# A fused 1-core fp32 block kernel: the orders of the mixer on VectorE and ScalarE, and output products taken ahead on two attention tiles

## The chip, the cores and the metric

The kernel runs on one core of one Trainium2 chip. The metric is device time in microseconds (us) of one execution; the number to compare is the median of several runs. A core has five engines with queues of their own: TensorE (PE in the profile; its weight loads are PEld), VectorE (DVE), ScalarE (ACT), GpSimd (POOL) and SyncE (SP, which here only issues DMAs). Each engine works through its queue in order; an instruction that waits for a semaphore holds back all that stands behind it on its engine.

## The reference

Two blocks in a row, all in float32, batch 1, 256 tokens, width 1024. The first block is a gated delta-net layer, a banded attention layer and two convolutional feed-forward layers. The second block, on which the change works, is one layer with a mixer and an MLP:

```
h = modulate(rmsnorm(x), sh1, sc1)
rq, rk, rv, rg, aq, ak, av = split(h @ w_in)            # w_in: 1024 x 2816
ret = silu(rg) * groupnorm(bidir_retention(rope(rq), rope(rk), rv)) * g   # 4 heads of 128
att = attention(rope(rms(aq)), [ctx keys, rope(rms(ak))], [ctx values, av])  # 8 heads of 64, 512 keys
x = x + g1 * (concat([ret, att]) @ w_out)               # w_out: 1024 x 1024
h2 = modulate(rmsnorm(x), sh2, sc2)
x = x + g2 * (relu(h2 @ w_ff1)**2 @ w_ff2)              # 1024 x 4096, 4096 x 1024
```

The result is a last rmsnorm of x.

## The kernel before

**Weights.** A weight matrix is cut in units of 128 x 1024 numbers (512 KB). For each unit SP issues a DMA into one of four `raw` slots; ACT copies it into one of four `wH` slots as fp32r (`hi`, L1362); DVE subtracts to get the remainder `wL` (`lo`, L2200). Every product is made of three matmuls, high x high, low x high and high x low (`three`, L607 to L609). `hi(c)` waits until PE has finished unit c - 4 (`unit_done`), and SP's DMA for unit c waits until `lo(c - 4)` is done. `ahead_hi(u)` and `ahead_lo(u)` are these two steps for unit u of the mixer, written by hand into the queues of ACT and DVE. Units 0 to 21 are `w_in`; units 22 to 29 are the eight units of `w_out` (`wo_c`, in the order of `OUT_UNITS`: pairs of bank j and half s, where s = 1 is the attention half of the rows of `w_out` and s = 0 the retention half); after them comes `w_ff1`.

**The mixer** (`win_pe`, `win_act`, `win_dve`) runs the projection with `w_in` and, between its units, four pairs of attention heads, p = 0 to 3, and four retention heads. One pair goes round the engines so: PE makes the scores (L1117); DVE takes the maxima (L2762); ACT the exponentials (L1725); DVE the reciprocals (L2771), and ACT and DVE each scale probabilities with them (L1732, L2775: `probabilities`); PE turns the probabilities (L1133, `att_turn`, 16 transposes); ACT and DVE copy them out of PSUM, ACT the upper and DVE the lower half (`probs_turned`: L1542 and L2780, into `stage` and `cv`); PE multiplies with the values (L1145, `att_y`); ACT and DVE split the result in high and low (`att_hi` L1542 into `yH`, `att_lo` L2200 into `zL`). DVE also makes the rotation of retention's keys and queries (`rotate`, L2743 to L2748), weights its scores (`ret_weights`, L2797) and sums its outputs (`ret_out`, L2802 to L2808), which PE makes in `ret_scores` (L1155) and `ret_outputs` (L1167, L1171).

**The end of the mixer.** Retention's outputs `o_r` get a group norm and the gate silu(rg) in `sg`. ACT: `ret_stats("square")` (L1763), the silu (L1856, which needs another activation table), `ret_stats("scale")` (L1765). POOL: an inverse root, the product of `sg` with the norm's gain in two parts (L2158), another inverse root. DVE: `last_stats`, `ret_stats("rows")` (L2829), `last_rows` (L2856). Then PE turns the rows (`ret_turn(0)` and `ret_turn(1)`, L1047) and ACT and DVE split them (`ret_hi`, `ret_lo`).

**The output product** (`mixer_out`) has eight units of 24 matmuls of 256 columns. `residual` (DVE, L2332, L2340) and `projected` (ACT, L1438) take each of its four banks, gate it and add it to x; `turn_pair` (PE, L769) turns two feature tiles of the new x, and ACT and DVE make `nH` and `nL` of them (L1383, L2253), the input of `w_ff1`. `OUT_DONE` says after how many units each bank is full. The first block of `w_ff1` (L1315 to L1317) waits for `nH` and `nL` pair by pair, and turns the fourth pair itself. The queue of PE, in order, ends the mixer with `att_turn(3)`, `att_y(3)`, then `mixer_out`.

Of the kernel before, what the change touches and what calls it, by code (L numbers as in the profile page):

```python
# [142 lines left out]
OUT_DONE = (3, 4, 6, 8)  # L143
OUT_UNITS = ((0, 1), (1, 1), (0, 0), (1, 0), (2, 1), (2, 0), (3, 1), (3, 0))
# [20 lines left out]
RET_OUT = (2, 2, 2, 1)  # L165
ATT_PAIR = ((4, 5), (6, 7))
# [66 lines left out]
def build(nc, a, out):  # L233
    with ExitStack() as ctx:
# [261 lines left out]
        s_tact = sem("s_tact")  # L496
        s_tdve = sem("s_tdve")
# [104 lines left out]
        def _(pe):  # L602
# [437 lines left out]
            def ret_turn(part):  # L1040

                pe.wait_ge(y_rows, part + 1)
                pe.wait_ge(m_od, 3 + part)
                for f in range(2):
                    for t in range(TT):
                        o = f * SEQ + t * P
                        tr = nc.tensor.transpose(ps[2 + part][:, o:o + P], o_r[:, t, DECAYS[2 * part + f]], ident)  # L1047
                tr.then_inc(y_pe, 1)

            def win_pe(X, C):  # L1050
# [85 lines left out]
                def att_y(p):  # L1136

                    pe.wait_ge(s_tact, 2 * p + 2)
                    pe.wait_ge(s_tdve, 2 * p + 2)
# [102 lines left out]
                att_turn(3)  # L1242
                att_y(3)

# [41 lines left out]
            win_pe(X, [xcH, xcL])  # L1286
            pe.wait_ge(m_od, RET_H)

            def mixer_out(x):
                b = {}  # L1290
                for u, (j, s) in enumerate(OUT_UNITS):
                    if u == 0:
                        pe.wait_ge(y_ready, RET_Y)
                    elif u == 2:
                        pe.wait_ge(y_ready, RET_Y + 2)
                    if s == 1:
                        b[j] = bank("wo_c", 0, j)
                    for t in range(TT):
                        token_half(b[j], 0, U("wo_c") + u, x, 1 - s, s, t)
                        if (u, t) == (0, 1):  # L1300
                            ret_turn(0)
                        elif (u, t) == (1, 0):
                            ret_turn(1)
                    if u in (4, 5, 7):
                        pair = (4, 5, 7).index(u)
# [45 lines left out]
        def _(act):  # L1351
# [65 lines left out]
            def projected(name):  # L1417
# [11 lines left out]
                for j in range(4):  # L1429
# [5 lines left out]
                    if j < 3:  # L1435
                        act.wait_ge(unit_done, U(name) + OUT_DONE[j])
                        act.wait_ge(unstaged, STAGED[name] + j - 1)
                        fn(stage[:, (STAGED[name] + j) % 2].rearrange("p a b -> p (a b)"), ps[(BANK[name] + j) % 4][:],  # L1438
                           ACT.Copy).then_inc(bank_free, 1)
                        ahead(0, U(name) + 2 * j)  # L1440
# [250 lines left out]
            def win_act():  # L1691
# [42 lines left out]
                def probs_turned(p):  # L1734
                    for g in range(2):
                        act.wait_ge(s_turn, 4 * p + 2 * g + 2)
                        cp(apT[g][:, 2:4].rearrange("p a b -> p (a b)"), ps[ATT_PAIR[g][1]][:]).then_inc(s_tact, 1)
# [1536 lines left out]
```

## Time and profile before

| | us |
|---|---|
| three runs | 1031.83, 1034.03, 1032.27 |
| median | 1032.27 |
| the profiled execution | 1034.53 |
| its span in the trace | 1032.7 |
| busy PE | 996.9 (97%) |
| busy DVE | 848.2 (82%) |
| busy ACT | 609.7 (59%) |
| busy POOL | 100.2 (10%) |

The time of the profiled execution is its span and 1.8 us around it. In the span the mixer's attention and retention lie at about 745 to 816 us, the output product at 816 to 842 us, `w_ff1` and `w_ff2` behind it. A row of the timeline gives the start, the busy time, the instruction, and in brackets how long the engine had been idle before it and what released it. The busy time of a matmul contains a modelled tail: matmuls of 256 columns start 0.12 us apart and show 0.28 us each, so a wait costs up to 0.16 us more than its bracket.

### The profile page before, as it was taken

The page shows a single profiled execution, that of the slowest core. Times are in us where ns is not written, and L with a number is a line of the kernel's source. Part 1 is how long each engine was busy: PE and PEld are TensorE (multiplying, and loading weights), DVE is VectorE, ACT ScalarE, POOL GpSimd, SP SyncE. Part 2 cuts the span into 40 slices and gives each one's busy share as a digit, 9 for nine tenths or more (in the row PEclk, how much of TensorE's full clock was granted, in tenths as well). Part 3 has the DMA queues.
Part 4 walks back from the last instruction along what each step waited for, and adds up shares of the span by engine and source line. Part 5 has one row for each costly group of instructions (what it writes and reads, how often), then busy time and mean ns, then how long its engine had stood idle before and what let it go on. Part 6 is the DMA issues. An engine that isn't in the chain of part 4 may idle for free.

```text
span 1032.7 us, 20800 instructions
## 1 busy us (share of the span) xinstructions
PE 996.9 (97%) x7662; PEld 925.4 (90%) x7662; DVE 848.2 (82%) x1566; ACT 609.7 (59%) x1056; POOL 100.2 (10%) x115
## 2 busy tenths in 40 slices
PE   6999999999999999998999999999998899999996
PEld 6999998999998889988999998888776799998884
DVE  5899888999889979887898899777788886668856
ACT  6697534766665564575766656556374565555443
POOL 1014422000000000001000001001200200000001
PEclk9999999999999999999999999999999999999998
DMA  9674313877776858737897757834422167766852
GB/s 292 171 212 154 103 55 104 247 210 211 224 213 217 292 165 266 268 100 235 224 274 208 220 185 257 272 100 135 132 70 75 42 162 206 221 196 220 278 149 116
DMA packets 216194, 193.09 MB, mean 187 GB/s; under 512 B 6032, under 2 KB 193568, under 8 KB 216000
## 3 DMA queue, kind: packets, MB, share of 16 engines
q1 hardware_dynamic: 206560, 158.09, 51.6%
q0 software_dynamic: 9136, 33.51, 9.8%
q8 instruction: 41, 0.67, 0.3%
q10 hardware_dynamic: 432, 0.61, 0.2%
q14 instruction: 25, 0.20, 0.1%
HBM read 191.14 MB, written 1.06 MB: 186 GB/s over the span
## 4 chain that ended last, share of the span: by engine, by line
PE 77%; DVE 12%; ACT 5%; DMA 3%; issue 2%; POOL 0%; POOLq 0%; ACTq 0%; DVEq 0%
PE ps L607 21%; PE ps L609 20%; PE ps L608 20%; DVE wL L2200 3%; PE ps L1316 3%; PE ps L1317 3%; PE ps L1315 3%; DMA modw<-in_w_mod_t 1%; DVE cv L3002 1%; PE ps L888 1%; ACT wH L1362 1%; DMA raw<-in_f_w_up 1%; PE ps L1145 1%; PE ps L875 1%; PE ps L784 1%
## 5 line engine op out<-in xcount | busy, mean ns | idle before, releaser
L1362 ACT ACTIVATE wH<-raw 128x1024 fp32r<-128x1024 f32 x298 | 313.5, 1062 | 260.4 <-PE ps L609 197.8
L2200 DVE TENSOR_TENSOR wL<-raw,wH 128x1024 fp32r<-128x1024 f32 x298 | 358.2, 1228 | 61.9 <-ACT wH L1362 61.0
L607 PE MATMUL ps<-yH,wH 128*128 128x256 f32 x704 | 195.3, 277 | 1.0 <-DVE yL L2253 1.0
L608 PE MATMUL ps<-yL,wH 128*128 128x256 f32 x704 | 194.4, 276 | 0.0
L609 PE MATMUL ps<-yH,wL 128*128 128x256 f32 x704 | 194.4, 276 | 0.0
L607 PEld LDWEIGHTS ps<-yH,wH 128*128 128x128 f32 x704 | 132.1, 188 | 1.3 <-DVE yL L2253 1.2
L608 PEld LDWEIGHTS ps<-yL,wH 128*128 128x128 f32 x704 | 132.2, 188 | 0.1
L609 PEld LDWEIGHTS ps<-yH,wL 128*128 128x128 f32 x704 | 132.1, 188 | 0.0
L607 PE MATMUL ps<-wH,aH 128*128 128x512 f32 (+1 forms) x308 | 119.4, 388 | 0.7 <-DVE aL L2200 0.6
L609 PE MATMUL ps<-wH,aL 128*128 128x512 f32 (+1 forms) x308 | 119.1, 387 | 0.0
L608 PE MATMUL ps<-wL,aH 128*128 128x512 f32 (+1 forms) x308 | 119.0, 386 | 0.0
L607 PE MATMUL ps<-wH,xH 128*128 128x256 f32 (+1 forms) x304 | 94.0, 309 | 3.2 <-DVE xL L2200 2.3
L608 PE MATMUL ps<-wL,xH 128*128 128x256 f32 (+1 forms) x304 | 91.6, 301 | 0.0
L609 PE MATMUL ps<-wH,xL 128*128 128x256 f32 (+1 forms) x304 | 91.6, 301 | 0.0
L3067 DVE SCALAR_TENSOR_TENSOR cv<-stage,cols,cv 128x254 f32<-128x254 f32 (+1 forms) x176 | 73.3, 481 | 1.5 <-ACT cv L1935 1.5
L607 PE MATMUL ps<-xH,wH 128*128 128x256 f32 x256 | 72.2, 282 | 0.8 <-DVE xL L2253 0.8
L1316 PE MATMUL ps<-nL,wH 128*128 128x256 f32 x256 | 72.6, 283 | 0.0
L1315 PE MATMUL ps<-nH,wH 128*128 128x258 f32 x256 | 72.2, 282 | 0.0
L1317 PE MATMUL ps<-nH,wL 128*128 128x258 f32 x256 | 72.1, 282 | 0.0
L608 PE MATMUL ps<-xL,wH 128*128 128x256 f32 x256 | 71.7, 280 | 0.0
L609 PE MATMUL ps<-xH,wL 128*128 128x256 f32 x256 | 71.7, 280 | 0.0
L2035 POOL DMA_DIRECT2D modw<-in_w_mod_t x48 | 25.9, 540 | 469.4 <-DVE modc L2222 326.8
(430 smaller groups left out, 2176.8 us busy)
## 6 DMA issues: line engine op xcount, KB each, us to landing
raw<-in_f_w_up SPq DMA_DIRECT2D x88, 512.0 KB, 5.0
raw<-in_w_ff SPq DMA_DIRECT2D x64, 512.0 KB, 4.7
modw<-in_w_mod_t POOLq DMA_DIRECT2D x48, 512.0 KB, 5.1
raw<-in_f_w_down SPq DMA_DIRECT2D x44, 512.0 KB, 4.4
raw<-in_a_w_in SPq DMA_DIRECT2D x32, 512.0 KB, 4.9
raw<-in_w_in SPq DMA_DIRECT2D x22, 512.0 KB, 3.8
raw<-in_w_kv SPq DMA_DIRECT2D x16, 512.0 KB, 5.4
raw<-in_a_w_out SPq DMA_DIRECT2D x8, 512.0 KB, 3.5
```

Of the source, the lines that this page charges most:

```text
L607: mm(o, l[0], r[0], start=first, stop=False, skip_group_check=check)
L608: mm(o, l[0], r[1], start=False, stop=False, skip_group_check=check)
L609: return mm(o, l[1], r[0], start=False, stop=last, skip_group_check=check)
L784: tr = nc.tensor.transpose(ps[first + k // 2][:, o:o + P], rows[:, t, k * P:(k + 1) * P], ident)
L875: tr = nc.tensor.transpose(ps[bank][:, x * P:(x + 1) * P], T_[:, 4 * g + x], ident)
L1315: mm(o[:, 0:SEQ + 2], w[0][:, k], nH[:, k, 0:SEQ + 2], start=k == 0, stop=False, skip_group_check=True)
L1316: mm(o[:, 0:SEQ], w[0][:, k], nL[:, k], start=False, stop=False, skip_group_check=True)
L1317: return mm(o[:, 0:SEQ + 2], w[1][:, k], nH[:, k, 0:SEQ + 2], start=False, stop=k == KD - 1, skip_group_check=True)
L1362: fn(slot(wH, c), raw[:, c % RAW], ACT.Copy).then_inc(hi_done, 1)
L2035: pool.dma_start(mod_tile(m), a["w_mod_t"][m * P:(m + 1) * P, :]).then_inc(mod_in[m % MOD_RING], 16)
L2200: return tt(o, x, hi.bitcast(F32), ALU.subtract)
L3067: c = stt(o[:, d:], x[:, 0:SEQ - d], w, o[:, d:], ALU.mult, ALU.add)
```

## The change

It changes no arithmetic, only orders, banks and which engine copies. Part by part:

- On DVE `probabilities(0)` stands before the rotation (`rotate(512, 0, 1)`), and `probabilities(2)` before `ahead_lo(22)`; on ACT `probabilities(2)` stands before `ahead_hi(23)`.
- For pair 1 ACT copies all four turned quarters; DVE copies none.
- On ACT the silu with its table load stands behind `ret_stats("square")` and `probs_turned(3)`; `ahead_hi(25)` stands before `att_hi(3)`, and `ahead_hi(26)` and `ahead_hi(27)` are taken into the mixer, before `ret_hi(0)` and `ret_hi(1)`. On DVE `ahead_lo(25)` stands before `last_rows`, `ahead_lo(26)` between `ret_lo(0)` and `ret_lo(1)`, and `ahead_lo(27)` behind them.
- On PE the first three units of `w_out` all belong to the attention half. Their products with the attention tiles that pairs 0 and 1 made (tiles 0 and 2 of the half: 12 of a unit's 24 matmuls) are taken ahead (`first_out`): one unit's before `att_y(3)`, two behind it. `mixer_out` makes the other half of each (tiles 1 and 3) and then the retention half, with new banks (`OUT_BANKS`, `RET_TURNED`) and new waits.
- The banks are full after 4, 5, 6 and 8 units (before: 3, 4, 6 and 8), and `turn_pair(0)` and `turn_pair(1)` each come one unit later.

```diff
-OUT_DONE = (3, 4, 6, 8)
-OUT_UNITS = ((0, 1), (1, 1), (0, 0), (1, 0), (2, 1), (2, 0), (3, 1), (3, 0))
+OUT_DONE = (4, 5, 6, 8)
+OUT_UNITS = ((0, 1), (1, 1), (2, 1), (0, 0), (1, 0), (2, 0), (3, 1), (3, 0))
+OUT_BANKS = (0, 2, 1, 3)
+OUT_AHEAD = ((6, 7), (8,), (9,))
+RET_TURNED = (5, 7)
...
+            def out_products(u, t, x, tiles):
+
+                j, s = OUT_UNITS[u]
+                w = [y.rearrange("p (k n) -> p k n", k=4) for y in w_unit(0, 8, U("wo_c") + u)]
+                for k in tiles:
+                    last = three(ps[OUT_BANKS[j]][:, t * 256:(t + 1) * 256],
+                                 [y[:, 4 * s + k, t * P:(t + 1) * P] for y in x], [y[:, k] for y in w],
+                                 s == 1 and t == 0 and k == 0, s == 0 and k == (1 if u == 3 else 3), check=True)
+                return last
+
+            def first_out(u, x):
+
+                for t in range(TT):
+                    out_products(u, t, x, (0, 2))
...
                 ret_outputs(3)
                 att_turn(3)
+                pe.wait_ge(m_od, 3)
+                pe.wait_ge(y_ready, ATT_Y + 4)
+                first_out(0, Z)
                 att_y(3)
+                first_out(1, Z)
+                pe.wait_ge(m_od, RET_H)
+                first_out(2, Z)
...
             def mixer_out(x):
...
+                pe.wait_ge(y_ready, RET_Y)
+                for u in range(3):
                     for t in range(TT):
+                        last = out_products(u, t, x, (1, 3))
+                        if (u, t) == (1, 1):
+                            last.then_inc(unit_done, 1)
                             ret_turn(0)
+                        elif (u, t) == (2, 0):
                             ret_turn(1)
+                    if u != 1:
+                        last.then_inc(unit_done, 1)
+                for part, tiles in ((0, (2, 3)), (1, (0, 1))):
+                    pe.wait_ge(y_ready, RET_Y + part + 1)
+                    for t in range(TT):
+                        last = out_products(3, t, x, tiles)
+                last.then_inc(unit_done, 1)
+                for u in range(4, 8):
+                    for t in range(TT):
+                        last = out_products(u, t, x, range(4))
+                    last.then_inc(unit_done, 1)
+                    if u >= 5:
+                        pair = u - 5
                         pe.wait_ge(unstaged, STAGED["wo_c"] + pair + 1)
                         turn_pair(pair, AUX + pair)
...
                 def probs_turned(p):
                     for g in range(2):
+                        if p == 1:
+                            act.wait_ge(s_turn, 4 * p + 2 * g + 1)
+                            cp(apT[g][:, 0:2].rearrange("p a b -> p (a b)"), ps[ATT_PAIR[g][0]][:]).then_inc(apt_low, 1)
                         act.wait_ge(s_turn, 4 * p + 2 * g + 2)
```

On VectorE, at the turned probabilities of pair 1: the queue before, from the end of the rotation of the first 128 tokens (`wt` and `qk_t` are its operands) to the next one.

```order
L2747 TENSOR_TENSOR qk_t<-qk_t,wt 128x4x64
L2748 TENSOR_TENSOR qk_t<-qk_t,wt 128x4x64
L2780 COPY stage<-ps 128x512
L2780 COPY cv<-ps 128x512
L2743 TENSOR_TENSOR wt<-qk_t,tb 128x256
```

The same place of the changed kernel:

```order
L2781 TENSOR_TENSOR qk_t<-qk_t,wt 128x4x64
L2782 TENSOR_TENSOR qk_t<-qk_t,wt 128x4x64
L2777 TENSOR_TENSOR wt<-qk_t,tb 128x256
L2778 TENSOR_TENSOR wt<-qk_t,tb 128x256
L2779 TENSOR_TENSOR qk_t<-qk_t,tb 128x4x64
```

The two copies are gone from DVE's queue; on ACT each of `stage` and `cv` is copied twice at that place.

On ScalarE, at the end of the mixer: before, from the last exponentials (`ap_`) on.

```order
L1725 ACTIVATE ap_,st_p<-ps,st_p 128x512 x2
L1856 ACT_TABLE_LOAD
L1856 ACTIVATE sg<-sg 128x1024
L1763 ACTIVATE rope,st_r<-o_r,st_r 128x128 x4
L1542 ACTIVATE stage<-ps 128x512
L1542 ACTIVATE cv<-ps 128x512
L1542 ACTIVATE yH<-ps 64x256 x2
L1362 ACTIVATE wH<-raw 128x1024
L1765 ACTIVATE o_r<-o_r,st_r 128x128 x4
L1542 ACTIVATE yH<-ps 128x512 x2
```

And in the changed kernel:

```order
L1795 ACTIVATE rope,st_r<-o_r,st_r 128x128 x4
L1571 ACTIVATE stage<-ps 128x512
L1571 ACTIVATE cv<-ps 128x512
L1890 ACT_TABLE_LOAD
L1890 ACTIVATE sg<-sg 128x1024
L1390 ACTIVATE wH<-raw 128x1024
L1571 ACTIVATE yH<-ps 64x256 x2
L1797 ACTIVATE o_r<-o_r,st_r 128x128 x4
L1390 ACTIVATE wH<-raw 128x1024
L1571 ACTIVATE yH<-ps 128x512
L1390 ACTIVATE wH<-raw 128x1024
L1571 ACTIVATE yH<-ps 128x512
```

The silu has moved behind the copies of the turned probabilities, and three weight copies now stand in front of splits (`yH`).

On TensorE, at the same time: before, from the last transposes of the probabilities (the names carry the bank numbers) on.

```order
L1133 MATMUL ps7<-cst,ap_ 128x128 x4
L1145 MATMUL ps4<-stage,cakv 64x256
L1145 MATMUL ps6<-cv,cakv 64x256
```

And in the changed kernel, where twelve rows of products with bank 0 lie between the transposes and `att_y(3)`, of which the first three and the last stand here:

```order
L1150 MATMUL ps7<-cst,ap_ 128x128 x4
L610 MATMUL ps0<-wH,yH 128x256
L611 MATMUL ps0<-wL,yH 128x256
L612 MATMUL ps0<-wH,zL 128x256
...
L612 MATMUL ps0<-wH,zL 128x256
L1162 MATMUL ps4<-stage,cakv 64x256
L1162 MATMUL ps6<-cv,cakv 64x256
```

What PE did last it does later now: `att_y(3)` stands behind half of unit 0's first pass.

## Rows read from the trace of the kernel before

**Rows 1.** Busy us (instructions) by stretch: PE, PEld, DVE, ACT, POOL; PE clock, DMA share, GB/s.
```profile
745.00:843.00 98.00, 90.12 (x653) 75.49 (x652) 78.76 (x162) 59.57 (x128) 5.39 (x4) 1.00 0.26 77
843.00:950.00 107.00, 107.00 (x838) 104.29 (x838) 75.18 (x139) 57.41 (x87) 3.83 (x5) 1.00 0.71 202
```
**Rows 2.** Timeline of PE, 749 to 830 us: each place where it stood idle.
```profile
754.62 1.97 PE L1133 MATMUL ps<-cst,ap_ 128*128 128x128 f32 x16 [0.68 <-ACT ap_ L1732]
...
779.04 0.40 PE L1145 MATMUL ps<-stage,cakv 128*64 128x256 f32 x1 [1.51 <-DVE cv L2780]
...
792.25 1.97 PE L1133 MATMUL ps<-cst,ap_ 128*128 128x128 f32 x16 [1.39 <-ACT ap_ L1732]
794.05 1.06 PE L1167 MATMUL ps<-rv,sT 128*128 128x128 f32 x8
...
808.95 1.97 PE L1133 MATMUL ps<-cst,ap_ 128*128 128x128 f32 x16 [0.31 <-DVE ap_ L2775]
812.71 0.43 PE L1145 MATMUL ps<-stage,cakv 128*64 128x256 f32 x1 [1.79 <-ACT cv L1542]
...
816.14 0.35 PE L607 MATMUL ps<-wH,yH 128*128 128x256 f32 x1 [1.49 <-issue]
816.33 0.28 PE L608 MATMUL ps<-wL,yH 128*128 128x256 f32 x1
816.46 0.28 PE L609 MATMUL ps<-wH,zL 128*128 128x256 f32 x1
...
829.58 0.35 PE L607 MATMUL ps<-wH,yH 128*128 128x256 f32 x1 [0.70 <-ACT stage L1438]
```
**Rows 3.** Timeline of DVE, 777 to 795 us: the copies of pair 1, the probabilities of pair 2.
```profile
778.22 0.68 DVE L2780 COPY cv<-ps 128x512 f32<-128x512 f32 x1
...
785.75 0.69 DVE L2791 COPY rqT<-ps 128x512 f32<-128x512 f32 x1 [0.88 <-PE ps L1095]
...
789.53 1.22 DVE L2200 TENSOR_TENSOR wL<-raw,wH 128x1024 fp32r<-128x1024 f32 x1
790.66 0.16 DVE L2771 RECIPROCAL st_p<-st_p 128x2 f32<-128x2 f32 x1
...
792.95 0.61 DVE L2808 SCALAR_TENSOR_TENSOR o_r<-ps,dec,o_r 128x128 f32<-128x128 f32 x2
```
**Rows 4.** Timeline of ACT, 774 to 813 us: pair 1's copies, pair 2's probabilities, the silu, pair 3's copies.
```profile
774.31 0.59 ACT L1542 ACTIVATE stage<-ps 128x512 f32<-128x512 f32 x1
...
777.56 0.60 ACT L1542 ACTIVATE sg<-ps 128x512 f32<-128x512 f32 x1 [1.23 <-PE ps L609]
...
790.85 1.34 ACT L1732 ACTIVATE ap_<-ap_,st_p 128x512 f32<-128x512 f32 x2 [0.58 <-DVE st_p L2771]
...
807.79 1.28 ACT L1856 ACT_TABLE_LOAD   x1
809.09 1.06 ACT L1856 ACTIVATE sg<-sg 128x1024 f32<-128x1024 f32 x1
...
812.07 0.58 ACT L1542 ACTIVATE cv<-ps 128x512 f32<-128x512 f32 x1
```
**Rows 5.** Timeline of DVE, 811 to 847 us: the end of the mixer and the last split.
```profile
811.03 0.68 DVE L2780 COPY cv<-ps 128x512 f32<-128x512 f32 x1
...
815.17 0.88 DVE L2200 TENSOR_TENSOR zL<-ps,yH 64x256 fp32r<-64x256 f32 x2 [0.18 <-ACT yH L1542]
...
819.04 1.14 DVE L2856 SCALAR_TENSOR_TENSOR o_r<-o_r,st_r,sg 128x128 f32<-128x128 f32 x4 [0.30 <-POOL st_r L2019]
820.09 1.22 DVE L2200 TENSOR_TENSOR wL<-raw,wH 128x1024 fp32r<-128x1024 f32 x1
...
822.19 0.69 DVE L2200 TENSOR_TENSOR zL<-ps,yH 128x512 fp32r<-128x512 f32 x1 [0.28 <-ACT yH L1542]
...
846.07 0.88 DVE L2253 SCALAR_TENSOR_TENSOR nL<-ps,gs,nH 128x256 fp32r<-128x256 f32 x2
```
**Rows 6.** Timeline of POOL, 813 to 818 us: the gain on the silu.
```profile
814.51 3.36 POOL L2158 TENSOR_TENSOR sg<-sg,rows_c 128x512 f32<-128x512 f32 x2
```

More of the change, by code:

```diff
@@ L1046, in ret_turn, with win_pe @@
                         o = f * SEQ + t * P
-                        tr = nc.tensor.transpose(ps[2 + part][:, o:o + P], o_r[:, t, DECAYS[2 * part + f]], ident)
+                        tr = nc.tensor.transpose(ps[RET_TURNED[part]][:, o:o + P], o_r[:, t, DECAYS[2 * part + f]], ident)
                 tr.then_inc(y_pe, 1)
-            def win_pe(X, C):
+            def out_products(u, t, x, tiles):
[9 more added lines that the diff above has]
+                    out_products(u, t, x, (0, 2))
+            def win_pe(X, C, Z):
                 bw = BANK["win"]
@@ L1437, in projected @@
                         act.wait_ge(unstaged, STAGED[name] + j - 1)
-                        fn(stage[:, (STAGED[name] + j) % 2].rearrange("p a b -> p (a b)"), ps[(BANK[name] + j) % 4][:],
+                        fn(stage[:, (STAGED[name] + j) % 2].rearrange("p a b -> p (a b)"), ps[OUT_BANKS[j]][:],
                            ACT.Copy).then_inc(bank_free, 1)
-                        ahead(0, U(name) + 2 * j)
+                        for c in OUT_AHEAD[j]:
+                            hi(0, 8, U(name) + c)
                     else:
@@ L1844, in win_act @@
                 exps(2, 0)
+                probabilities(2)
                 ahead_hi(23)
-                probabilities(2)
                 ahead_hi(24)
@@ L2340, in residual @@
                     tt(hc, hc, s, ALU.add).then_inc(unstaged, 1)
-                    if j < 3:
-                        ahead(0, U(name) + 2 * j)
+                    for c in OUT_AHEAD[j] if j < 3 else ():
+                        lo(0, 8, U(name) + c)
                     if j == 1:
@@ L2888, in win_dve @@
                 ahead_lo(17)
+                probabilities(0)
                 dve.wait_ge(bank_free, bw + 11)
                 rotate(512, 0, 1)
-                probabilities(0)
                 ahead_lo(18)
@@ L2917, in win_dve @@
                 ret_weights(1)
+                probabilities(2)
                 ahead_lo(22)
-                probabilities(2)
                 ret_out(0)
@@ L2937, in win_dve @@
                 ret_stats("rows")
+                ahead_lo(25)
                 last_rows()
-                ahead_lo(25)
                 ret_lo(0)
+                ahead_lo(26)
                 ret_lo(1)
+                ahead_lo(27)
             def by_tiles(gate):
```

44 lines of the change are left out of this document (15 added, 29 removed).

## The prediction

> **What bounds the kernel now.** I read the busy times by stretch first. PE is busy in all 107 us of the stretch behind the mixer and the output product, and in 90.1 of the 98 us of the mixer and the output product themselves, at a granted clock of 1.00, which is 2.4 GHz, in both [rows 1]. So PE sets the time, and what can be won without less work is the idle time between 745 and 843 us. The timeline of PE shows where it lies [rows 2]: seven places, with brackets of 0.68, 1.51, 1.39, 0.31, 1.79, 1.49 and 0.70 us, 7.9 us together, which is all but 0.1 us of the idle time in the window (98.00 - 90.12 = 7.88). Each bracket names an order on ACT or DVE: something less urgent stood before the instruction that PE needed. As PE never waits in the next 107 us, whatever PE gains here moves all that follows, and the weights, since their transfers are released by PE's progress through `unit_done` and `lo_done`; I take it through to the end at full value.
>
> How to price one wait: where the same kind of matmul goes on, it costs its bracket and the 0.16 us of modelled tail (starts 0.12 us apart, 0.28 us shown). Where PE changes into or out of `att_y`, the change alone costs about as much, and I take the bracket.
>
> **The change part by part.**
>
> *Pair 0.* The reciprocals come before a rotation of six instructions, so ACT's scaled probabilities are there before the products with `ckv` end, and the 0.68 us wait goes: 0.68 + 0.16 = 0.84. The rotation that steps back is needed by PE only for the transposes at some 766 us, and what DVE did next was a weight split; nothing is late in its place.
>
> *Pair 1.* The wait of 1.51 us at 779.04 ends with DVE's copy into `cv`, 778.22 + 0.68 = 778.90 [rows 2, 3]. That copy stood behind a rotation. On ACT the four copies cost at most 4 x 0.6 = 2.4 us from 774.31 [rows 4], so the last ends before 776.7, and PE is ready at 779.04 - 1.51 = 777.5: hidden with 0.8 us to spare. Behind them on ACT come one weight copy and the copy of `sg`, which had 1.23 us of idle time before it [rows 4], as much as the two new copies take. All 1.5 us are won.
>
> *Pair 2.* The wait of 1.39 us at 792.25 costs 1.39 + 0.16 = 1.55. DVE split a weight unit (789.53) before its reciprocal (790.66): 1.13 us [rows 3]. With the order turned, ACT's two scalings start 1.13 us earlier than 790.85 [rows 4], the transposes at 791.12, and end at 792.92. But PE's next step, `ret_outputs(1)` (794.05 in the rows, directly behind the transposes), needs DVE's `ret_out(0)`, which ends at 792.95 + 0.61 = 793.56 [rows 3] and does not move, since the weight split is only put behind the reciprocals and still lies before it. So PE starts it at about 793.6 instead of 794.05 [rows 2]: of 1.13 us only 0.45 arrive, and a new wait of 0.6 us for `o_r` appears. That DVE is otherwise no further behind is seen in its own wait for PE of 0.88 us just before [rows 3]: it moves with PE.
>
> *Pair 3, before the transposes* (0.31 us): scores, maxima and exponentials keep their order; it stays.
>
> *Pair 3, behind the transposes.* PE waits 1.79 us, until 812.71, for ACT's copy that starts at 812.07 [rows 2, 4]. ACT had loaded a table for 1.28 us, made the silu for 1.06 us and then four squares. DVE's own copy, 811.03 + 0.68 = 811.71 [rows 5], is the next that is late: moving the silu alone wins 1.0. With `first_out(0)` PE has 12 matmuls x 0.12 = 1.4 us of products at hand from 810.75 to 812.2, and DVE's copy is hidden too. Won: 1.7. The 1.28 us and 1.06 us of the silu now start at about 811.5, so `sg` is ready at 813.9. POOL takes it at 814.51 [rows 6], behind an inverse root of its own: 0.6 us of slack, so it costs nothing.
>
> Here a rule of the Trainium skill speaks against the change. The table load of 1.28 us ends at 809.07, and the silu starts at 809.09 [rows 4]: nothing lies between. "ScalarE: Activation LUTs", section "Rules for kernel authors", wants about 2.7 us counted for each switch to another table set; by it the silu would be ready 1.4 us later, POOL 0.8 us later, and the sum below about 0.3 us smaller. The row decides.
>
> *The seam into the output product.* PE waits 1.49 us at 816.14 for the end of DVE's split, 815.17 + 0.88 = 816.05 [rows 2, 5]. With `first_out(1)` and `first_out(2)`, 24 x 0.12 = 2.8 us, PE is busy until about 817. Won: 1.5.
>
> *The bank wait at 829.58* (0.70 + 0.16 = 0.86): PE waited because units 26 and 27 were split only after the first bank had been staged. They are now split in the mixer. Won: 0.86.
>
> *What it costs.* (a) Three more changes between kinds of matmul: the first of a kind starts its successor 0.19 us later instead of 0.12 (816.14 to 816.33, against 816.33 to 816.46 [rows 2]), and the change itself about 0.1: 0.4 together, between 0.2 and 0.8. (b) `ahead_lo(25)` now stands before `last_rows`, which therefore end at 819.04 + 1.14 + 1.1 = 821.3 instead of 820.2 [rows 5]; PE arrives at `ret_turn(1)` at about 821.2 (808.95 + 1.8 transposes + 1.4 + 1.9 `att_y` + 2.8 + 3.6 products of the second pass + 0.4 turn + 0.3 changes). So 0.2, between 0 and 1. Behind it, `ret_lo(1)` ends about 823.4 (before: 822.88 [rows 5]), with one more weight split in front of it, and PE needs it at 823.7. (c) Banks 0 and 1 are full, and turned, one unit later (24 x 0.12 = 2.8 us), so ACT and DVE carry four banks' work in less time before the first block of `w_ff1`. The last `nL` was done at 846.07 + 0.88 = 846.95 [rows 5], just when PE came to it. I give it 0.4, between 0 and 2.
>
> **The sum.** 0.84 + 1.5 + 0.45 + 1.7 + 1.5 + 0.86 = 6.85 won, 0.4 + 0.2 + 0.4 = 1.0 lost: 5.8 us faster. Against the profiled execution, 1034.53 - 5.8 = 1028.7; that one is 2.3 us over the median, so against the median 1032.27 - 5.8 = **1026.5 us**.
>
> **Rivals.**
>
> *DVE becomes the bound at the end of the mixer.* For it: from 809 to 823 us DVE has only brackets of 0.18, 0.30 and 0.28 us [rows 5], it gets one weight split more before `ret_lo(1)`, and PE has only 0.3 us of slack to it. Each us by which `last_rows`, POOL's product or the front of `w_ff1` is later is a us lost. With the upper ends of (a), (b) and (c), 0.8 + 1 + 2 instead of 1.0, the gain is 3.0: **1029.3 us**.
>
> *More goes than I count.* Pair 2's new wait and the 0.31 us of pair 3 vanish because DVE has two copies (1.2 us) less to do, and (b) and (c) cost nothing: 6.85 + 1.1 + 0.3 - 0.3 = 8.0: **1024.3 us**.
>
> *The gain stays in the mixer.* If transfers, not PE, paced `w_ff1` (DMA share 0.71 [rows 1]), PE would wait there for what it gained. Against it: no idle time at all in that stretch. It would give **1031 us**, no change to be told.
>
> *Slower, by one thing in PE's queue.* `ret_turn(1)` waits for `last_rows`, and behind it on PE stand half a unit of ready products and all of unit 3. `last_rows` now stand behind `ahead_lo(25)`, that behind ACT's `ahead_hi(25)`, and this behind the silu. Each us that this chain is late beyond 821.2 stops PE for one us. It must be 5.8 + 2.1 = 7.9 us late before the kernel is slower than can be told, 1034.5 us or more. For it: four engines meet there. Against it: the pieces are single rows of 1.0 to 1.2 us, and unit 25's weights come long before.
>
> **How the numbers follow.** Forecast (gain 4 to 7.4) 0.60; DVE bound at the end (gain 2.1 to 4) 0.15; more goes 0.12; the gain stays in the mixer, or is eaten up, 0.08; slower 0.05. A measurement of this kernel can tell some 0.2%, 2.1 us, from no change. So faster 0.87, same 0.08, slower 0.05. The range that holds 8 in 10 reaches from a gain of 8.3 to one of 2.3: 1024.0 to 1030.0.
>
> **What would show it.** In the changed profile: no wait for `cv` from DVE at the `att_y` of pair 1; at pair 2 a shorter wait for `ap_` and a new one of about 0.6 us for `o_r` before `ret_outputs(1)`; products with `yH` between the last transposes and `att_y(3)`, and no wait before either; no wait for ACT's `stage` in the output product; perhaps 0.2 us before `ret_turn(1)` and 0.4 us for `nL` in the first block of `w_ff1`. The stretch behind stays fully busy. The prediction would be wrong if PE waits over 1 us at `ret_turn(1)`, at unit 3 or at the front of `w_ff1`, or if idle time shows up in `w_ff1` or `w_ff2` where there was none.

## The result, and the profile after

| | before | after |
|---|---|---|
| median of the runs beside each other, us | 1032.75 (4 runs) | 1027.18 (4 runs) |
| lowest and highest | 1031.83 and 1034.03 | 1026.71 and 1027.98 |
| ratio after to before, 95% interval | | 0.994 (0.9929 to 0.9952) |
| the profiled execution | 1034.53 | 1027.24 |
| its span | 1032.7 | 1025.4 |

The kernel is 5.6 us, 0.5 to 0.7%, faster; 1026.5 us was predicted. A second, later set of runs gave 1025.95 us (6 runs) against 1033.23 (11 runs), a ratio of 0.9931 (0.9918 to 0.9945).

The busy times by stretch of the changed kernel answer to [rows 1] (columns as there):

```profile
745.00:843.00 98.00, 96.81 (x718) 82.84 (x715) 84.08 (x172) 64.51 (x140) 7.59 (x5) 1.00 0.30 89
843.00:950.00 107.00, 107.00 (x806) 102.89 (x806) 75.13 (x137) 56.88 (x82) 2.88 (x6) 1.00 0.73 215
```

Of 7.88 us of idle PE 1.19 us are left, and the stretch behind is as full as before. The timeline of PE in the changed kernel, in answer to [rows 2]:

```profile
787.52 1.97 PE L1150 MATMUL ps<-cst,ap_ 128*128 128x128 f32 x16 [0.25 <-ACT ap_ L1761]
790.12 1.13 PE L1184 MATMUL ps<-rv,sT 128*128 128x128 f32 x8 [0.63 <-DVE o_r L2842]
...
805.09 1.97 PE L1150 MATMUL ps<-cst,ap_ 128*128 128x128 f32 x16 [0.30 <-DVE ap_ L2809]
806.81 0.37 PE L610 MATMUL ps<-wH,yH 128*128 128x256 f32 x1
...
808.40 0.43 PE L1162 MATMUL ps<-stage,cakv 128*64 128x256 f32 x1
...
810.27 0.38 PE L610 MATMUL ps<-wH,yH 128*128 128x256 f32 x1
...
817.20 0.60 PE L1049 MATMUL ps<-cst,o_r 128*128 128x128 f32 x4
...
838.90 0.38 PE L1343 MATMUL ps<-nH,wH 128*128 128x258 f32 x1
...
846.14 0.59 PE L630 MATMUL ps<-rd,cst 128*128 128x256 f32 x2
```

Three brackets are left in this stretch, and all three were named in the prediction: 0.25 (the shorter wait of pair 2), 0.63 (the new one for `o_r`) and 0.30 us (pair 3, which stays). The products with `yH` stand at 806.81 and 810.27, before and behind `att_y(3)`, without a bracket.

**A ruler for all runs.** Executions differ by a us or more in places that the change doesn't touch: the scores of pair 0 begin at 745.44 us before, at 744.33 after, and at 745.36 in a second profile of the changed kernel. So I measure from there in two pieces: **A**, from the first scores of pair 0 (L1117, L1134) to the transposes of pair 3 (L1133, L1150), and **B**, from these to the transposed roots in the first block of `w_ff1` (L627, L630). Before, A runs from 745.44 to 808.95 [rows 2] and B to 854.26; after, from 744.33 to 805.09 and 846.14.

| kernel | A, us | B, us | A + B | against after | median of its runs | ratio to before (95%) |
|---|---|---|---|---|---|---|
| before | 63.51 | 45.31 | 108.82 | +7.01 | 1032.75 to 1033.4 (five sets) | |
| after | 60.76 | 41.05 | 101.81 | | 1027.18 | 0.994 (0.9929 to 0.9952) |
| `e11_changed_again` | 60.76 | 41.06 | 101.82 | +0.01 | 1025.95 | 0.9931 (0.9918 to 0.9945) |
| `e1_orders` | 60.76 | 46.68 | 107.44 | +5.63 | 1031.14 | 0.9979 (0.9968 to 0.9989) |
| `e2_products` | 63.46 | 41.52 | 104.98 | +3.17 | 1029.97 | 0.9972 (0.9961 to 0.9983) |
| `e3_silu` | 60.75 | 41.51 | 102.26 | +0.45 | 1027.14 | 0.9947 (0.9932 to 0.9962) |
| `e4_seam` | 60.76 | 41.70 | 102.46 | +0.65 | 1027.69 | 0.9946 (0.9931 to 0.9961) |
| `e5_sum` | 59.89 | 41.08 | 100.97 | -0.84 | 1025.38 | 0.9937 (0.9919 to 0.9954) |
| `e6_rows` | 60.75 | 41.70 | 102.45 | +0.64 | 1027.13 | 0.9944 (0.9927 to 0.9961) |
| `e7_splits` | 60.76 | 46.50 | 107.26 | +5.45 | 1031.69 | 0.9987 (0.9975 to 0.9999) |
| `e8_copies` | 62.33 | 41.10 | 103.43 | +1.62 | 1027.64 | 0.9951 (0.9934 to 0.9968) |
| `e9_late_rows` | 60.76 | 44.60 | 105.36 | +3.55 | 1028.81 | 0.9958 (0.9944 to 0.9973) |
| `e10_combined` | 59.64 | 41.79 | 101.43 | -0.38 | 1025.59 | 0.993 (0.9917 to 0.9943) |
| `e12_pair2` | 59.80 | 41.08 | 100.88 | -0.93 | 1025.49 | 0.9927 (0.9913 to 0.9942) |

Two executions of the same kernel agree within 0.01 us on this ruler, while their medians differ by 1.2 us. Effects under 1 us are therefore read from A and B, not from the times; each kernel but the changed one has a single profile. Behind B, from the transposed roots to the last unit's first matmul, all twelve later profiles take 164.71 to 164.72 us. Only before (165.29) and after (166.03) lose time there. In the profile of after it is one wait in `w_ff2`, behind weights that came late (ACT had waited 1.42 us for their transfer):

```profile
1006.42 0.46 PE L610 MATMUL ps<-wH,aH 128*128 128x512 f32 x1 [0.85 <-DVE aL L2234]
```

Idle time in `w_ff2` was named in the prediction as a sign of being wrong. But `e11_changed_again`, the same kernel, has none there, so the 0.7 us that the profile of after loses against before at that place is not put down to the change.

### The profile page after: what moved, and what is told of

It is laid out like the page before. It is cut to its first block, busy times and chain, and to the rows that moved or that the text cites. A ratio compares the mean times of both kernels' runs of the same rounds, so it can differ in the third digit from the quotient of the medians.

```text
span 1025.4 us, 20797 instructions
## 1 busy us (share of the span) xinstructions
PE 996.5 (97%) x7662; PEld 925.3 (90%) x7662; DVE 846.8 (83%) x1564; ACT 609.4 (59%) x1058; POOL 100.9 (10%) x115
## 4 chain that ended last, share of the span: by engine, by line
PE 81%; DVE 10%; ACT 4%; DMA 2%; issue 2%; POOL 0%; POOLq 0%; ACTq 0%; DVEq 0%; SPq 0%
PE ps L610 21%; PE ps L611 21%; PE ps L612 21%; PE ps L1344 3%; DVE wL L2234 3%; PE ps L1343 3%; PE ps L1345 3%; DVE cv L3037 1%; PE ps L891 1%; DMA raw<-in_w_ff 1%; ACT wH L1390 1%; PE ps L878 1%; PE ps L1162 1%; DMA modw<-in_w_mod_t 1%; PE ps L787 1%
```

## The experiments

**Each part alone.** `e1_orders` is the kernel before with the new orders on DVE and ACT and nothing else; `e2_products` is the changed kernel with the old orders, which leaves the products ahead, the banks and the early splits. The diff is that of `e2_products` against the changed kernel, first on ACT, then on DVE; `e1_orders` makes the opposite edits in the kernel before.

```diff
                 def probs_turned(p):
-                        if p == 1:
-                            act.wait_ge(s_turn, 4 * p + 2 * g + 1)
-                            cp(apT[g][:, 0:2].rearrange("p a b -> p (a b)"), ps[ATT_PAIR[g][0]][:]).then_inc(apt_low, 1)
...
-                probabilities(2)
                 ahead_hi(23)
+                probabilities(2)
...
-                ret_stats("square")
-                probs_turned(3)
                 act.wait_ge(bank_free, bw + WIN_FILLS)
                 fn(sg[:], sg[:], ACT.Silu).then_inc(sg_act, 1)
+                ret_stats("square")
+                probs_turned(3)
...
-                probabilities(0)
                 dve.wait_ge(bank_free, bw + 11)
                 rotate(512, 0, 1)
+                probabilities(0)
...
                 rotate(0, 0, 3)
+                probs_turned(1)
...
-                probabilities(2)
                 ahead_lo(22)
+                probabilities(2)
```

> The kernel before with the changes of order on DVE and ACT alone (probabilities of pairs 0 and 2, pair 1's copies on ACT, the silu behind the last copies); no products ahead, old order of units. Main theory (each term is a wait of its own, and they add up): pair 0 wins 0.85 us, pair 1 1.6 us, pair 2 0.35 us with a new wait of about 0.6 us for o_r. At att_y(3) the wait of 1.79 us shrinks to about 0.8 us, since DVE's copy is the next that is late. The 1.49 us at the seam and the 0.70 us for ACT's stage stay. In all 3.8 us faster than before: about 1029.0 us where before is 1032.7. Rival (DVE's lower load is what pays, and the products ahead only hide what is left): the seam and the stage wait shrink too, and the gain is 5 us or more. Rival (orders on DVE and ACT win nothing by themselves, since the end of the mixer is bound by the norm's chain): under 2 us.

A is 2.75 us shorter, to the hundredth what the changed kernel gains there. But B is 1.37 us longer than before, where it should have been 1.0 us shorter. PE's timeline of this kernel:

```profile
806.72 0.40 PE L1145 MATMUL ps<-stage,cakv 128*64 128x256 f32 x1 [0.94 <-DVE cv L2783]
...
810.86 0.55 PE L607 MATMUL ps<-wH,yH 128*128 128x256 f32 x1 [2.19 <-issue]
811.21 0.41 PE L608 MATMUL ps<-wL,yH 128*128 128x256 f32 x1
811.42 0.41 PE L609 MATMUL ps<-wH,zL 128*128 128x256 f32 x1
```

And DVE's, for the split that the seam waits for:

```profile
809.88 0.88 DVE L2203 TENSOR_TENSOR zL<-ps,yH 64x256 fp32r<-64x256 f32 x2
```

Two things are seen. First, the wait at `att_y(3)` did shrink by 0.85 us (1.79 to 0.94), and the wait at the seam grew by 0.70 us (1.49 to 2.19). DVE stands in one unbroken chain there (copies, `ret_out(3)`, `last_stats`), and its split has no bracket: it ends 6.95 us behind the start of pair 3's transposes, before it was 7.10 (808.95 to 816.05 [rows 2, 5]). PE only changed where it waits for it. Second, behind the wait of 2.19 us the matmuls start 0.21 us apart instead of 0.12. The busy times by stretch show why:

```profile
811.00:814.20 3.20, 3.20 (x16) 3.20 (x17) 2.33 (x4) 1.65 (x4) 3.09 (x2) 0.50 0.01 3
```

The granted clock is 0.50, that is 1.2 instead of 2.4 GHz, for 3.2 us. From the seam to `ret_turn(0)` the same 24 products take 4.43 us, before 2.92 (816.14 to 819.06): 1.5 us lost. The 0.70 us for ACT's `stage` stays, as expected. So the orders alone keep 1.4 us of their 3.8 in the profile, and 2.3 us in the medians.

> The changed kernel with the old orders on DVE and ACT for pairs 0, 1 and 2 and the silu in its old place; products taken ahead and the early splits of units 25 to 27 stay. Main theory: the waits of 0.68, 1.51 and 1.39 us of pairs 0 to 2 are back (together 2.8 us of cost), and at att_y(3) about 0.45 us of the old 1.79 is left, since the 1.4 us of first_out(0) cover the rest; seam and stage wait stay away. 3.2 us slower than the changed kernel, 3.0 us faster than before: about 1029.8 us where before is 1032.7. Rival (the two parts depend on each other: with 1.2 us more to do, DVE becomes the bound at the end): waits at ret_turn(1) or at unit 3 appear, and the gain over before is under 2 us.

Confirmed: 3.17 us of cost against 3.2 expected. A loses 2.70, and B 0.47, which is one wait. PE's waits of this kernel, 740 to 850 us (total us, times, longest):

```profile
PE ps L1150 <- ACT ap_ L1761: 2.1, 2, 1.4
PE ps L1162 <- DVE cv L2811: 1.5, 1, 1.5
PE ps L1162 <- ACT cv L1571: 0.4, 1, 0.4
PE ps L1150 <- DVE ap_ L2806: 0.3, 1, 0.3
```

No wait at `ret_turn(1)` or unit 3: DVE's load is not what decides there. The two parts don't add up to the whole: with the products ahead, the new orders are worth 3.17 us; without them 1.38 (108.82 - 107.44). The difference of 1.8 us arises at the end of the mixer: 1.5 of it is the fall of the clock behind the longer wait at the seam, which one profile of `e1_orders` shows. The rest is the wait at `att_y(3)`: with the products ahead the orders win 0.47 us there, without them the seam takes back all but 0.15 (7.10 - 6.95).

**The silu's place.**

```diff
-                ret_stats("square")
-                probs_turned(3)
                 act.wait_ge(bank_free, bw + WIN_FILLS)
                 fn(sg[:], sg[:], ACT.Silu).then_inc(sg_act, 1)
+                ret_stats("square")
+                probs_turned(3)
```

> The changed kernel with one thing undone: on ACT the silu and its table load stand again before the squares and the copies of pair 3. Main theory: ACT's copy into cv then ends at about 808.8 us instead of 807.7, and PE comes to att_y(3) at 808.4: a wait of 0.45 us, 0.4 us slower than the changed kernel, since first_out(0) covers 1.4 of the old 1.79 us by itself. Rival (the silu's place is what wins the wait): 1.5 us or more slower. Rival (nothing, the silu's early end helps POOL and with it last_rows): equal or faster.

0.45 us, as expected: one wait more, for ACT's `cv` at `att_y(3)`.

```profile
808.03 0.43 PE L1162 MATMUL ps<-stage,cakv 128*64 128x256 f32 x1 [0.37 <-ACT cv L1571]
```

Of the old 1.79 us the products ahead cover 1.4 by themselves, and the silu's move only the rest.

**Half the cover at the seam.**

```diff
                 first_out(1, Z)
                 pe.wait_ge(m_od, RET_H)
-                first_out(2, Z)
...
-                        last = out_products(u, t, x, (1, 3))
+                        last = out_products(u, t, x, (0, 2, 1, 3) if u == 2 else (1, 3))
```

> The changed kernel with only one unit's ready products (first_out(1)) between att_y(3) and the wait for pair 3's split; those of unit 2 are made in mixer_out. Main theory (12 products cover 1.42 us): in the changed kernel DVE's split ends at 812.4 us and PE comes to it at 813.1; here PE comes at 811.7 and waits 0.7 us, with the modelled tail 0.85 us of cost, and all later work is that much later: 0.8 us slower than the changed kernel. Rival (PE has slack behind it, because it waits for the rows of the norm anyway): no slower.

0.65 us slower, with this row on PE:

```profile
813.78 0.36 PE L610 MATMUL ps<-wH,yH 128*128 128x256 f32 x1 [0.54 <-issue]
```

The direction and mechanism hold, the size is 0.2 us under. The products of both units at the seam are needed, and together they have some 0.8 us to spare (PE is through them at 813.2, DVE's split at 812.4).

**What held pair 2 back.**

```diff
                 probabilities(2)
-                ahead_lo(22)
                 ret_out(0)
+                ahead_lo(22)
```

> The changed kernel with ret_out(0) moved ahead of the split ahead_lo(22) on DVE. In the changed kernel PE waits 0.63 us for o_r before ret_outputs(1), and nothing else lies between. Main theory (of pair 2's gain 0.8 us is held back by that split, which stands before ret_out(0)): the wait goes, with its tail 0.8 us faster from the transposes of pair 2 to those of pair 3. Rival (something else, such as ret_weights(1) or a bank, is late just behind): a wait of some 0.5 us with another name, and under 0.3 us won. From the transposes of pair 3 to the turned reciprocal root in the first block of w_ff1 no change, 41.05 us.

0.87 us less in A, B unchanged (41.08). Only two waits are left between 740 and 850 us:

```profile
PE ps L1150 <- DVE ap_ L2809: 0.3, 1, 0.3
PE ps L1150 <- ACT ap_ L1761: 0.2, 1, 0.2
```

So the split in front of `ret_out(0)` was what kept 0.8 us of pair 2's gain, as the prediction had it, and moving it costs nothing that A or B shows.

**`last_rows` before the split of unit 25.**

```diff
-                ahead_lo(25)
                 last_rows()
+                ahead_lo(25)
```

> The changed kernel with last_rows ahead of ahead_lo(25) on DVE, as in the kernel before. The prediction took 0.2 us for this place, between 0 and 1. Main theory after the changed kernel's trace (PE comes to ret_turn(1) at 817.20 us, last_rows end at 817.05): no change, since PE doesn't wait there, and the split of unit 25 ends about 817.1, 1.2 us before PE needs it. Rival (the rows are late and the trace doesn't show it): 0.2 us faster or more. Rival (the split of unit 25 is needed earlier): slower, with a wait for DVE's wL at unit 25.

It is 0.64 us slower. Only the last rival had the direction, and it named another wait: PE does stop at unit 3 of `w_out` (unit 25 of the mixer's count), but for `zL`, the split of the retention rows, not for `wL`.

```profile
819.12 0.39 PE L610 MATMUL ps<-wH,yH 128*128 128x256 f32 x1 [0.18 <-DVE zL L2234]
```

The timeline of DVE in this kernel:

```profile
816.19 1.14 DVE L2890 SCALAR_TENSOR_TENSOR o_r<-o_r,st_r,sg 128x128 f32<-128x128 f32 x4 [0.90 <-POOL st_r L2053]
817.25 1.22 DVE L2234 TENSOR_TENSOR wL<-raw,wH 128x1024 fp32r<-128x1024 f32 x1
818.39 0.68 DVE L2234 TENSOR_TENSOR zL<-ps,yH 128x512 fp32r<-128x512 f32 x1
```

In the changed kernel:

```profile
814.79 1.22 DVE L2234 TENSOR_TENSOR wL<-raw,wH 128x1024 fp32r<-128x1024 f32 x1
815.92 1.13 DVE L2890 SCALAR_TENSOR_TENSOR o_r<-o_r,st_r,sg 128x128 f32<-128x128 f32 x4
817.32 0.69 DVE L2234 TENSOR_TENSOR zL<-ps,yH 128x512 fp32r<-128x512 f32 x1 [0.26 <-ACT yH L1571]
```

`last_rows` need POOL's second root, and without the split DVE stands idle for it for 0.90 us. The split fills that hole. Put behind the rows, it pushes both `ret_lo` back, and PE gets the bracket of 0.18 us at unit 3 and a second gap too short for one (0.33 instead of 0.12 us between two starts, at 820.86). The place that the prediction booked as a cost of 0.2 us is worth 0.6.

**Without the early splits of units 26 and 27.**

```diff
-OUT_AHEAD = ((6, 7), (8,), (9,))
+OUT_AHEAD = ((4, 5), (6, 7), (8, 9))
...
-                ahead_hi(26)
-                ahead_hi(27)
...
-                ahead_lo(26)
-                ahead_lo(27)
```

> The changed kernel without the splits of units 26 and 27 in the mixer: ACT and DVE make them only after the first bank is staged, as in the kernel before. The prediction counted this part at 0.86 us, which is what the wait was with the old order of units. Main theory (the new order needs it more: bank 0 is now full after four units instead of three, so PE has no unit of 2.8 us left to hide the staging and the split of unit 26): PE waits 0.70 + 2.8 = 3.5 us before unit 26, 3.6 us slower than the changed kernel. A wait as long as that may bring the granted clock down behind it, which would cost 1 to 2 us more. Rival (it is worth what it cured): 0.9 us slower.

PE's row and the stretch behind it:

```profile
823.71 0.39 PE L610 MATMUL ps<-wH,yH 128*128 128x256 f32 x1 [3.44 <-DVE wL L2232]
```
```profile
823.70:827.20 3.50, 3.49 (x19) 3.50 (x20) 1.09 (x1) 0.00 (x0) 0.00 (x0) 0.61 0.60 164
```

The wait is 3.44 us (3.5 expected), and the clock fell behind it, to a mean of 0.61 in this stretch. Together 5.45 us, of it 3.6 for the wait, about 1.5 for the clock and 0.3 for one more gap (831.02 to 831.69). Without these splits next to nothing of the change is left (0.9987). What the prediction counted as one more saving of 0.86 us is a condition of the new order of units.

**Pair 1's copies back on DVE.**

```diff
                 rotate(0, 0, 3)
+                probs_turned(1)
...
-                        if p == 1:
-                            act.wait_ge(s_turn, 4 * p + 2 * g + 1)
-                            cp(apT[g][:, 0:2].rearrange("p a b -> p (a b)"), ps[ATT_PAIR[g][0]][:]).then_inc(apt_low, 1)
```

> The changed kernel with pair 1's two copies (stage, cv lower halves) back on DVE behind the rotation, one each on the two engines. Main theory (the copies stand behind a rotation, 1.5 us too late, and DVE catches up in its waits for PE): a wait of 1.5 us for DVE's cv at att_y(1), 1.6 us slower, and nothing else changes. Rival (DVE is close to being the bound, so 1.2 us more of work in it costs elsewhere too): 2 us slower or more, with longer waits for DVE at pair 2 and 3.

1.62 us, of it 1.57 in A, by one wait of 1.5 us for DVE's `cv`; all other waits are those of the changed kernel. The rival of a DVE near its limit has nothing for it.

**The slower rival, made on purpose.**

```diff
                 ahead_lo(25)
+                sq = rope[:, 0, 512:]
+                for _ in range(3):
+                    st.do(tt(sq, sq, sq, ALU.max))
                 last_rows()
```

> The changed kernel with three more operations on DVE (128x512, 0.6 to 0.7 us each, on a scratch region, no result used) between ahead_lo(25) and last_rows: the chain of the slower rival made late on purpose. Main theory (PE has 0.15 us of slack at ret_turn(1), and the splits behind it none): last_rows end 1.9 us later, PE waits 1.8 us before ret_turn(1), and the whole is 1.9 us slower than the changed kernel; if the granted clock falls behind that wait, 1 to 2 us more. Rival (the half unit and unit 3 behind it can't be moved, but the later units catch up): under 1 us slower.

```profile
819.81 0.80 PE L1049 MATMUL ps<-cst,o_r 128*128 128x128 f32 x4 [1.92 <-DVE o_r L2890]
```
```profile
820.20:823.70 3.50, 3.50 (x19) 3.50 (x18) 3.02 (x4) 0.60 (x1) 0.00 (x0) 0.52 0.15 43
```

PE waited 1.92 us at `ret_turn(1)`, and the clock fell behind it: 3.55 us in the profile, 2.9 us in the medians against the changed kernel's runs on the same chip (`e11_changed_again`), 1.6 against its first set. The three operations took 2.1 us (816.44 to 818.58), and they arrive at PE as a wait of about that length, so the rival's slope was right at this point, and more is lost once the clock falls. In the changed kernel `last_rows` end at 817.05 us and PE comes at 817.20, 0.15 us of slack. One step on there is none: `ret_lo(1)`, the second split of the retention rows, ends at 819.74 (819.06 + 0.68), and PE's products with it start at 819.80, 0.15 instead of 0.12 us behind their predecessor. So the rival stood at its starting point. Yet 2 us of delay did not make the kernel slower than before (1028.81 us).

**What is left, taken away.** `e10_combined`:

```diff
-                ret_weights(1)
                 probabilities(2)
-                ahead_lo(22)
+                ret_weights(1)
                 ret_out(0)
+                ahead_lo(22)
...
-                        for g in (1,) if p < 3 else (0, 1):
+                        for g in (0, 1) if (p, t) == (3, 1) else (1,):
...
-                def probabilities(p):
-                    for t in (1, 0):
+                def probabilities(p, tiles=(1, 0)):
+                    for t in tiles:
...
                 exps(3, 0)
+                probabilities(3, (0,))
                 ret_stats("square")
```

> The changed kernel with what is left of its waits taken away: on DVE ret_out(0) ahead of ahead_lo(22), and probabilities(2) ahead of ret_weights(1); of pair 3's last two scalings ACT makes one (before, DVE made all four). Main theory: the waits of 0.63 us for o_r, 0.25 us for ap_ of pair 2 and 0.30 us for ap_ of pair 3 all go or shrink to under 0.1 us: 0.8 + 0.35 + 0.3 = 1.4 us faster than the changed kernel, about 7.5 us faster than before (1025.5 us where before is 1033). Rival (with pair 2 earlier DVE's ret_weights(1), now behind the probabilities, is late for ret_outputs(1)): only 0.8 to 1 us. Rival (ACT's squares of the norm, 0.6 us later, delay its copies of pair 3 or the mean's chain): the seam waits again.

> The changed kernel itself, beside the combined one on the same chip, so that the two are compared directly. From the scores of pair 0 to the turned root in the first block of w_ff1 it should take 101.8 us again, the combined one 100.4; before them and behind them only what differs from execution to execution.

A falls by 1.12 us, and B grows by 0.73. PE's row:

```profile
816.98 0.65 PE L1049 MATMUL ps<-cst,o_r 128*128 128x128 f32 x4 [0.61 <-DVE o_r L2891]
```

This is the slower rival again, in small. DVE's and POOL's rows ahead of it (the second is the product of `sg`: shortest, median and longest time of its two parts, in ns, and their starts):

```profile
811.31 1.00 DVE L2858 TENSOR_TENSOR st_r<-st_r 128x4 f32<-128x4 f32 x1
```
```profile
L2193 POOL TENSOR_TENSOR sg<-sg,rows_c x2: 1295/1458/1622, 809.4 to 811.0; 128x512 f32<-128x512 f32 x2
```

An operation on four columns, 0.14 to 0.31 us in the thirteen other profiles, took 1.00 and ended at 812.31; POOL's second part ran from 811.0 in 1.295 us and ended there too. The last kernel is the same without the change to pair 3:

> The combined kernel without its change to pair 3, so that the squares of the norm on ACT stay where the changed kernel has them: on DVE ret_out(0) ahead of ahead_lo(22), probabilities(2) ahead of ret_weights(1). Main theory (in the combined kernel ACT's extra scaling pushed the norm's chain back, and the rows came 0.6 us late): from the scores of pair 0 to the transposes of pair 3 59.5 us, from there to the turned root 41.05 us as in the changed kernel, 100.6 us together, with only the 0.30 us for pair 3's ap_ left as a wait; 1.2 us faster than the changed kernel in that stretch, and 0.8 us faster than the combined one. Rival (DVE's operation that took 1.00 instead of 0.14 us beside POOL's product is what cost, and it comes by chance or with pair 2's order): a wait of about 0.6 us at ret_turn(1) is there too, and no more than 0.4 us is won.

B is 41.08 again, as the main theory had it, and the wait at `ret_turn(1)` is gone. A is 59.80 instead of 59.5: a wait of 0.15 us for `o_r` is left beside the 0.30. A + B is 100.88, 0.93 us under the changed kernel (1.2 expected). The same rows:

```profile
811.69 0.14 DVE L2857 TENSOR_TENSOR st_r<-st_r 128x4 f32<-128x4 f32 x1
```
```profile
L2192 POOL TENSOR_TENSOR sg<-sg,rows_c x2: 1617/1799/1981, 810.0 to 811.6; 128x512 f32<-128x512 f32 x2
```

Here DVE isn't held up, and POOL's slower part takes 1.981 us, 0.69 us more than the short one above, which is the length of DVE's next operation (0.68 us). So in each of the two profiles one engine is held up by the other: in the combined kernel DVE until POOL's part ends, here POOL by the length of DVE's operation. That fits what the Trainium skill says ("SBUF — State Buffer", section "SBUF: two separate sides"): an operation of GpSimd and one of DVE with two inputs from SBUF lock the port pair that they share, whichever starts first holds it for its whole instruction, and the other blocks. Who was first isn't read off the records: by them POOL's second part starts ahead of DVE's operation in both kernels, by 0.27 us in the combined one (811.04 and 811.31) and by 0.04 us here (811.65 and 811.69), and starts on POOL are rough.

My reason for `e12_pair2`, that ACT's extra scaling pushed the norm's chain back, is not borne out: POOL's first root starts 4.31 us behind the transposes of pair 3 in the combined kernel and 4.55 in this one, so it is earlier, not later. DVE's operation stands at the same distance in both (7.22 and 7.23 us), since it comes behind the split of pair 3's result. With one scaling fewer on DVE, POOL thus moved 0.24 us ahead against it, which is how the change to pair 3 can bring the two together. Whether it always does, or this execution happened on it, stays open: one profile shows it.

The best of these, `e12_pair2` (1025.49 us) and `e5_sum` (1025.38 us), beat the changed kernel by 0.8 to 0.9 us on the ruler. Their ratios to before, 0.9927 and 0.9937, overlap that of the changed kernel, so the times alone can't tell them apart.

## Why the prediction was right, and where it wasn't

The total, 5.8 us predicted, 5.6 us measured in the medians and 7.0 on the ruler, came by the mechanism that was named: waits in the mixer that other engines ended too late. That 5.8 lies so near to 5.6 is luck, since the second set of runs gives 7.3. Against the ruler the prediction is 1.2 us short, 0.8 of it in the costs and 0.34 in the tail of pair 3's wait. By its steps:

| step | predicted, us | on the ruler, us |
|---|---|---|
| pair 0 | 0.84 | 0.85 |
| pair 1 | 1.5 | 1.59 |
| pair 2 | 0.45, new wait 0.6 | 0.35, new wait 0.63 |
| pair 3, behind the transposes | 1.7 | 2.04 |
| seam | 1.5 | 1.56 |
| bank wait | 0.86 | 0.86 (bracket and tail; gone) |
| costs (a), (b), (c) | -1.0 | -0.2 (what is left of 7.0) |

*The idle time.* The seven brackets make 7.87 us, which is all of it (7.88), not all but 0.1.

*Pairs 0 to 2.* From the scores to the transposes of pair 0 it is 9.18 us before and 8.33 after; from the scores of pair 1 to those of pair 2 19.79 and 18.20; from there to the transposes of pair 2 1.15 us less, of which 0.80 is given back before `ret_outputs(1)`. `e5_sum` shows that the reason given for that was the right one.

*Pair 3.* The wait went whole, tail and all: 3.76 us from the transposes to the next matmul before, 1.72 after (805.09 to 806.81). I had left the tail out, by the rule that a change into `att_y` costs as much. The two changes around the products ahead cost 0.2 together: `first_out(0)` takes 1.59 us for 12 x 0.118 = 1.42 us of products. That is cost (a).

One remark was wrong: that "moving the silu alone wins 1.0". At that wait it nearly does (0.85 in `e1_orders`), but 0.70 of it comes back at the seam. Nothing in the sum hung on it, since the products ahead cured both; still, the view to read would have been DVE's timeline [rows 5], whose 0.18 us of idle time before the split say that the seam goes by DVE.

*The silu and POOL.* The rows of the changed kernel:

```profile
809.00 1.06 ACT L1890 ACTIVATE sg<-sg 128x1024 f32<-128x1024 f32 x1
```
```profile
810.65 3.56 POOL L2192 TENSOR_TENSOR sg<-sg,rows_c 128x512 f32<-128x512 f32 x2
814.32 1.42 POOL L2053 TENSOR_TENSOR st_r<-st_r,mhalf 128x4 f32<-128x4 f32 x1
```

The silu starts 0.01 us behind its table load (807.71 + 1.28 and 809.00) and ends at 810.06; POOL takes `sg` at 810.65, behind its own root. So 0.59 us of slack, against 0.6 predicted. The Trainium skill ("ScalarE: Activation LUTs", section "Rules for kernel authors") counts about 2.7 us for the switch. An estimate by that figure: POOL 0.8 us later, its second root ended at 816.5 instead of 815.7, and `last_rows` some 0.5 us behind PE, where the prediction gave 0.3 without a working. The trace shows the load's 1.28 us and nothing else.

*The costs* are where the sum was off: 1.0 booked, 0.2 found. (a) 0.2 instead of 0.4. (b) Nothing: `last_rows` end 0.15 us before PE comes, and the split put in front of them lies in a hole of DVE that POOL makes (`e6_rows`). The step that failed is the count of DVE's queue from row to row without POOL's root. The prediction put the whole split, 1.1 us, on top of the old end of `last_rows`; behind the transposes of pair 3 they end at 11.96 us instead of 11.23, 0.73 later, and with the rows in front of the split they would end at 11.82 (`e6_rows`). So most of the 0.73 is POOL's: it takes `sg` at the same distance as before (5.56 us), but its second root ends at 10.65 instead of 10.05 us. The product takes 3.56 instead of 3.36 us [rows 6] and the root 1.42 instead of 1.01, which in the kernel before was

```profile
817.99 1.01 POOL L2019 TENSOR_TENSOR st_r<-st_r,mhalf 128x4 f32<-128x4 f32 x1
```

Why POOL takes longer stays open. (c) 0.16 us: matmuls that start 0.12 us apart have one gap of 0.28 (838.62 to 838.90), where `nL` was ready at 838.85. Against (a) and (c) stands a gap of the kernel before that the prediction hadn't seen: at its first retention unit two starts lay 0.27 us apart (822.67 and 822.94), in the changed kernel 0.15 (819.65 and 819.80).

*The bank wait* was right in size and wrong in kind: 3.6 us hang on the early splits, not 0.86, because the same change lets bank 0 be full one unit later (`e7_splits`).

*Rivals.* DVE as the bound: no, `e8_copies` gives it 1.2 us more to do, `e2_products` as well, and it costs only the waits themselves. The gain that stays in the mixer: no, 107.00 of 107 us busy behind it, and from the roots to the last unit none of the twelve later profiles takes longer than before (164.71 against 165.29). The slower one: its slope is real (`e9_late_rows`), it stood at its starting point, with 0.15 us of slack at `ret_turn(1)` and none at unit 3. More than counted: its costs were small, as it said, but pair 2's new wait and pair 3's 0.30 us stayed.

## What to carry to other kernels

When several waits of one engine lie in a row, ask for each what the releaser itself waits for: a wait that is cured moves PE forward to the next one, and if that one's releaser works without a break, the gain stops there; ready work of PE's own, put into the gap, passes both. Where units of work are put in another order, count again when their operands have to be there, since a preparation that used to save a little may become what the order stands on. And compare kernels whose effects are under 1 us by fixed marks in the trace around the change, where repeats agree to 0.01 us, not by medians, which here differ by 1.2 us between two sets of one kernel.

## What the runs showed of the hardware

The granted clock can fall from 2.4 to 1.2 GHz behind a single wait of PE, and stays there for about 3.4 us (810.85 to 814.26 us in `e1_orders`), which costs about 1.5 us. It fell behind all three waits of 1.92, 2.19 and 3.44 us at the end of the mixer, and behind none of the waits up to 1.79 us there. In another place, at about 168 us, all fourteen profiles have the same wait of 1.34 us (with one of 0.33 us 2 us ahead of it), and behind it the clock fell in three of them (`e4_seam`, `e8_copies`, `e9_late_rows`). The same stretch in `e4_seam`:

```profile
168.00:171.50 3.50, 3.50 (x19) 3.50 (x19) 2.31 (x12) 0.09 (x1) 1.64 (x1) 0.52 0.02 5
```

and in `e5_sum`, where the wait ends at nearly the same time (167.59 us, against 167.64) and the clock did not fall:

```profile
168.00:171.50 3.50, 3.50 (x32) 3.50 (x31) 2.31 (x10) 0.05 (x1) 1.64 (x1) 1.00 0.00 0
```

19 matmuls against 32 in the same time. A wait near 2 us was thus worth nearly twice its length in `e9_late_rows` and `e1_orders`. A fall that comes in some executions and not in others can also be part of why runs of one kernel differ by 1 to 3 us, but that is not shown: of 50 runs of the kernel before, the 11 with a granted clock of 0.995 or less took 1034.1 us in the mean and the other 39 took 1032.9, and within both groups the times scatter further.
